# MLP up units in pairs by Strassen's scheme, with block sums of weights and tokens made on the chip

## The reference, cut to what matters

```python
def sqrelu_mlp(x, w_up, w_down):
    return jnp.square(jax.nn.relu(x @ w_up)) @ w_down
...
h = h + sqrelu_mlp(rmsnorm_2(h, mlp_norm[l]), w_up[l], w_down[l])
```

## Time and profile before

| | |
|---|---|
| median of 3 runs | 2758.52 us (2756.25 to 2761.14) |
| the profiled execution | 2754.03 us, its span 2752.3 us |
| granted TensorE clock | 0.998 of full speed |
| busy: PE, DVE, ACT, POOL | 99%, 44%, 39%, 48% |
| an up unit: 24 matmuls of 512 tokens | 5.44 us |
| a quarter of an MLP: 16 units | 87 us |
| HBM | 94 GB/s over the span |

### The profile page before, as it was taken

The page is one execution under the profiler, slowest core; times in us unless marked ns, Lnnn a source line. Parts: engine busy times, 40 slices in busy tenths (PEclk is TensorE's granted clock), DMA queues, the critical chain, the costliest instruction groups (busy, mean ns, idle before and its releaser), DMA issues.

```text
span 2752.3 us, 34320 instructions
## 1 busy us (share of the span) xinstructions
PE 2713.0 (99%) x12422; PEld 2208.7 (80%) x12422; DVE 1220.6 (44%) x1603; ACT 1062.5 (39%) x1566; POOL 1321.0 (48%) x1028
## 2 busy tenths in 40 slices
PE   9999999999999999999999999999999998999999
PEld 7777777888877788787888877788888876788887
DVE  6755555212258645555121268633324237443222
ACT  4444434322343444434222348423324338433222
POOL 5455445544464544455544465454444432354443
PEclk9999999999999999999999999999999999999999
DMA  4333322233332333322333322222233220223233
GB/s 144 93 102 97 99 92 84 93 100 97 95 101 94 98 100 100 100 92 85 96 96 100 99 93 92 90 94 99 92 99 122 85 77 16 69 92 100 93 97 99
DMA packets 72699, 259.16 MB, mean 94 GB/s; under 512 B 8192, under 2 KB 9088, under 8 KB 72448
## 3 DMA queue, kind: packets, MB, share of 16 engines
q1 hardware_dynamic: 71280, 254.17, 29.0%
q10 hardware_dynamic: 1296, 3.28, 0.3%
HBM read 255.31 MB, written 2.10 MB: 94 GB/s over the span
## 4 chain that ended last, share of the span: by engine, by line
PE 79%; DVE 7%; issue 6%; POOL 5%; ACT 2%; DMA 1%; POOLq 0%; DVEq 0%; SPq 0%
PE ps L902 25%; PE ps L904 24%; PE ps L903 24%; POOL w_lo L370 3%; POOL w_lo L368 2%; PE ps L1143 1%; DVE XS L1954 1%; DVE fb L1953 1%; ACT w_hi L433 1%; PE ps L1038 1%; DVE st L1518 1%; PE ps L1029 1%; PE ps L1387 1%; PE ps L1389 1%; PE ps L1388 1%
## 5 line engine op out<-in xcount | busy, mean ns | idle before, releaser
L368 POOL TENSOR_TENSOR w_lo<-w_raw,w_hi 128x512 fp32r<-128x512 f32 x476 | 631.5, 1327 | 1330.8 <-ACT w_hi L433 1330.2
L902 PE MATMUL ps<-H_hi,w_hi 128*128 128x512 f32 x2240 | 890.0, 397 | 12.2 <-POOL w_lo L370 5.7
L904 PE MATMUL ps<-H_hi,w_lo 128*128 128x512 f32 x2240 | 872.5, 390 | 0.0
L903 PE MATMUL ps<-H_lo,w_hi 128*128 128x512 f32 x2240 | 872.3, 389 | 0.0
L433 ACT ACTIVATE w_hi<-w_raw 128x1024 fp32r<-128x1024 f32 x476 | 499.6, 1055 | 556.1 <-DMA w_raw<-w_all 556.0
L370 POOL TENSOR_TENSOR w_lo<-w_raw,w_hi 128x512 fp32r<-128x512 f32 x476 | 655.1, 1376 | 0.0
L902 PEld LDWEIGHTS ps<-H_hi,w_hi 128*128 128x128 f32 x2240 | 420.6, 188 | 116.4 <-issue 13.4
L903 PEld LDWEIGHTS ps<-H_lo,w_hi 128*128 128x128 f32 x2240 | 420.7, 188 | 92.2 <-issue 7.4
L904 PEld LDWEIGHTS ps<-H_hi,w_lo 128*128 128x128 f32 x2240 | 420.5, 188 | 88.3
L902 PE MATMUL ps<-Y_hi,w_hi 128*128 128x512 f32 x1168 | 457.2, 391 | 7.5 <-DVE Y_lo L1666 2.8
L904 PE MATMUL ps<-Y_hi,w_lo 128*128 128x512 f32 x1168 | 454.7, 389 | 0.0
(11 more groups left out here) (278 smaller groups left out, 2477.7 us busy)
## 6 DMA issues: line engine op xcount, KB each, us to landing
w_raw<-w_all SPq DMA_DIRECT2D x476, 512.0 KB, 3.5
X<-xT SPq DMA_DIRECT2D x8, 256.0 KB, 5.5
rel_bias<-bias ACTq DMA_DIRECT2D x1, 2048.0 KB, 8.4
outT<-X SPq DMA_DIRECT2D x8, 256.0 KB, 3.2
sguw<-sgu_wT ACTq DMA_DIRECT2D x2, 256.0 KB, 3.1
CS<-cossin SPq DMA_DIRECT2D x1, 256.0 KB, 7.5
sgub<-sgu_b ACTq DMA_DIRECT2D x2, 128.0 KB, 3.0
sgug<-sgu_g ACTq DMA_DIRECT2D x2, 128.0 KB, 3.0
```

Source lines behind the costliest of these rows:

```text
L368: nc.gpsimd.tensor_tensor(w_lo[:, s, 0:UNIT // 2], w_raw[:, s, 0:UNIT // 2], f(w_hi[:, s, 0:UNIT // 2]), ALU.subtract).then_inc(w_lo_half, 1)
L902: MM(out, wh, xh, start=start, stop=False)
L903: MM(out, wh, xl, start=False, stop=False)
L904: return MM(out, wl, xh, start=False, stop=stop)
```

## The change

It pairs the up units. The tokens are cut into two halves of 256 (columns 1 and 2), the inputs into two halves of 512, and two up units are the two blocks of output features. For the pair, a 2 x 2 block product, eight half products (512 inputs, 128 features, 256 tokens) become seven, by the scheme with 15 block sums:

- Token sums (four blocks `T` of 512 inputs x 256 tokens, gain included) are made once for each MLP: `tokens_split` on ACT and `token_sums` on DVE after the output units, then `T_hi` on ACT (four instructions of 1024 columns), `T_lo` two on DVE and two on POOL.
- Weight sums (four of 512 columns for each pair: S1, S2, S4, S3, in two sets of buffers `E_raw`, `E_hi`, `E_lo`) are made on DVE by `weight_sum`, up to two pairs ahead, rounded on ACT by `hi_sum`, and their rest is made on POOL in `low_pair`, behind three halves of the pair's own weights. The fourth half is used only in sums.
- PE's `window` makes the seven products of 12 matmuls of 256 tokens: G, r, V (S1), r resumed (S2), then the cross product of the next pair (bank 4), V resumed (S4), r resumed (S3). Resuming adds on to a bank whose content has been copied out before: ACT copies four half banks (`copied`).
- DVE's `c11`, `c12` and `c2` add copies and banks to the four output blocks in `fa`; `linear` is ReLU and the factor `RS` in one instruction, ACT squares twice (to `XS`, and rounded to `Y_hi`), and DVE subtracts (`low`).

The cross product of a pair waits for `c11` of the pair before it, since they share bank 4. In the first quarter of each MLP the first four up units stay as they were, and pairs 2 and 3 follow. All else, down units included, stays, but the down units take the tiles of `Y` in the order in which they are now made.

```diff
+            def low_pair(n, U0, i, p):
+                u, q, c = unit_of(U0, i, 2 * p), pair_of(n, i, p), U0 + 2 * p
+                s2, s1 = c % WSLOTS, (c + 1) % WSLOTS
+                eng.wait_ge(w_hi_ready, u + 2)
+                eng.wait_ge(st_sum, q * 4 + 3)
+                nc.gpsimd.tensor_tensor(w_lo[:, s1, S:UNIT], w_raw[:, s1, S:UNIT], f(w_hi[:, s1, S:UNIT]), ALU.subtract).then_inc(w_lo_half, 1)
+                eng.wait_ge(st_sum, q * 4 + 4)
+                nc.gpsimd.tensor_tensor(w_lo[:, s2, S:UNIT], w_raw[:, s2, S:UNIT], f(w_hi[:, s2, S:UNIT]), ALU.subtract).then_inc(w_lo_half, 1)
+                nc.gpsimd.tensor_tensor(w_lo[:, s1, 0:S], w_raw[:, s1, 0:S], f(w_hi[:, s1, 0:S]), ALU.subtract).then_inc(w_lo_ready, 1)
+                for n_, o in enumerate((S1_, S2_, S4_, S3_)):
+                    if n_ < 3:
+                        eng.wait_ge(st_hi, q * 3 + (n_ + 1))
+                    nc.gpsimd.tensor_tensor(sums_of(E_lo, p, o), sums_of(E_raw, p, o), f(E_hi[:, p % 2, o:o + 1, :]),
+                                            ALU.subtract).then_inc(st_lo if n_ else w_lo_ready, 1)
...
+                for t in (1, 2):
+                    eng.wait_ge(t_hi, 4 * n + (3 if t == 1 else 4))
+                    nc.gpsimd.tensor_tensor(T_lo[:, t, :, :], T_raw[:, t, :, :], f(T_hi[:, t, :, :]), ALU.subtract).then_inc(t_lo_g, 1)
...
+                act.wait_ge(t_sum, n + 1)
+                for t in (3, 0, 1, 2):
+                    nc.scalar.activation(T_hi[:, t, :, :], T_raw[:, t, :, :], ACT.Copy).then_inc(t_hi, 1)
...
+                def ahead(i, p, part):
+                    if p < 4:
+                        if part == 0:
+                            hi_second(i, p)
+                        else:
+                            hi_first(i, p)
+                            hi_sum(i, p, S1_)
+                            hi_sum(i, p, S2_)
+                    elif p == 4:
+                        split_weights(unit_of(U0, i, 8 + part), U0 + 8 + part)
+                def window(i, p, first):
+                    if first:
+                        hi_second(i, p + 1)
+                        hi_first(i, p + 1)
+                        copied(i, p, COPY_G)
+                        copied(i, p, COPY_R1)
+                        hi_sum(i, p + 1, S1_)
+                        hi_sum(i, p + 1, S2_)
+                        copied(i, p, COPY_V)
+                        hi_sum(i, p + 1, S4_, 2)
+                    else:
+                        squared(i, p - 1, 0)
+                        copied(i, p, COPY_G)
+                        copied(i, p, COPY_R1)
+                        squared(i, p - 1, 1)
+                        copied(i, p, COPY_V)
+                        if p + 1 < 4:
+                            hi_sum(i, p + 1, S4_, 2)
+                    ahead(i, p + 2, 0)
+                    copied(i, p, COPY_R2)
+                    ahead(i, p + 2, 1)
...
+                def quarter(i, last):
+                    if first_pair(i):
+                        for j in range(4):
+                            u = U0 + j
+                            if j == 1:
+                                tick(u)
+                            elif j == 2:
+                                hi_second(i, 2)
+                                hi_first(i, 2)
+                            elif j == 3:
+                                hi_sum(i, 2, S1_)
+                                hi_sum(i, 2, S2_)
+                                hi_sum(i, 2, S4_, 2)
+                            act.wait_ge(w_used, u + 1)
...
+                def cross(i, p):
+                    u, q = unit_of(U0, i, 2 * p), pair_of(n, i, p)
+                    pe.wait_ge(w_lo_half, u + 1)
+                    if not isinstance(q, int) or q:
+                        pe.wait_ge(st_c, q * 2 - 1)
+                    half_product(BANK_Q, *slot_part(U0 + 2 * p + 1, 1), *half_of_h(4, 0))
...
+                def window(i, p, first):
+                    u, q = unit_of(U0, i, 2 * p), pair_of(n, i, p)
+                    r = bank_r(U0, p)
+                    if first:
+                        cross(i, p)
+                    pe.wait_ge(w_lo_half, u + 2)
+                    half_product(BANK_G, *slot_part(U0 + 2 * p, 1), *tokens(3)).then_inc(w_used, 1)
+                    pe.wait_ge(w_lo_ready, u + 1)
+                    pe.wait_ge(unit_out, u - 2)
+                    half_product(r, *slot_part(U0 + 2 * p + 1, 0), *half_of_h(0, 0)).then_inc(w_used, 1)
+                    pe.wait_ge(w_lo_ready, u + 2)
+                    if not isinstance(q, int) or q:
+                        pe.wait_ge(st_c, q * 2)
+                    half_product(BANK_V, *sum_part(p, S1_), *tokens(0)).then_inc(st_mm, 1)
+                    pe.wait_ge(st_lo, q * 3 + 1)
+                    pe.wait_ge(st_copy, q * 4 + 2)
+                    half_product(r, *sum_part(p, S2_), *tokens(1), fresh=False).then_inc(st_mm, 1)
+                    if p + 1 < 4:
+                        cross(i, p + 1)
+                    pe.wait_ge(st_lo, q * 3 + 2)
+                    pe.wait_ge(st_copy, q * 4 + 3)
+                    half_product(BANK_V, *sum_part(p, S4_), *half_of_h(4, 1), fresh=False).then_inc(st_mm, 1)
+                    pe.wait_ge(st_lo, q * 3 + 3)
+                    pe.wait_ge(st_copy, q * 4 + 4)
+                    half_product(r, *sum_part(p, S3_), *tokens(2), fresh=False).then_inc(st_mm, 1)
...
+            def token_sums(n, k):
+                g1, g2 = v(f"mlp{n}", k), v(f"mlp{n}", k + 4)
+                early, late = X[:, k + 4, 0:HS], X[:, k + 4, HS:S]
+                dve.wait_ge(t_raw, 4 * n + k + 1)
+                link(VE.scalar_tensor_tensor(T_raw[:, 0, k, :], X[:, k, HS:S], g1, T_raw[:, 0, k, :], ALU.mult, ALU.subtract))
+                VE.scalar_tensor_tensor(T_raw[:, 2, k, :], late, g2, T_raw[:, 2, k, :], ALU.mult, ALU.subtract)
+                link(VE.scalar_tensor_tensor(T_raw[:, 1, k, :], late, g2, T_raw[:, 0, k, :], ALU.mult, ALU.subtract))
+                i = VE.scalar_tensor_tensor(T_raw[:, 3, k, :], early, g2, T_raw[:, 1, k, :], ALU.mult, ALU.subtract)
+                if k == 3:
+                    i.then_inc(t_sum, 1)
...
+                    if not isinstance(q, int) or q >= 2:
+                        dve.wait_ge(st_mm, q * 4 + (o - 7))
+                    if o == S1_:
+                        dve.wait_ge(*loads(unit_of(U0, i, 2 * p), c))
+                        x = VE.tensor_tensor(s1, a21, a22, ALU.add)
+                    elif o == S2_:
+                        dve.wait_ge(*loads(unit_of(U0, i, 2 * p + 1), c + 1))
+                        dve.wait_ge(st_sum, q * 4 + 1)
+                        x = VE.tensor_tensor(s2, s1, a11, ALU.subtract)
+                    elif o == S4_:
+                        dve.wait_ge(st_sum, q * 4 + 2)
+                        x = VE.tensor_tensor(sums_of(E_raw, p, S4_), a12, s2, ALU.subtract)
+                    else:
+                        x = VE.tensor_tensor(sums_of(E_raw, p, S3_), a11, a21, ALU.subtract)
+                    x.then_inc(st_sum, 1)
...
+                def c11(i, p):
+                    q = pair_of(n, i, p)
+                    dve.wait_ge(st_copy, q * 4 + 2)
+                    VE.tensor_tensor(fa[:, 0, 0:HS], ps[:, BANK_Q, 0:HS], cp[:, COPY_R1, :], ALU.add).then_inc(st_c, 1)
...
+                    VE.scalar_tensor_tensor(fb[:, a, :], fa[:, a, :], 0.0, RS[:], ALU.max, ALU.mult).then_inc(st_lin, 1)
...
+                def window(i, p, first):
+                    if first:
+                        for o in (S1_, S2_, S4_, S3_):
+                            weight_sum(i, p + 1, o)
+                        c11(i, p)
+                    else:
+                        c2(i, p - 1)
+                        if p + 1 < 4:
+                            weight_sum(i, p + 1, S3_)
+                        linear(i, p - 1, 1)
+                        low(i, p - 1, 0)
+                        c11(i, p)
+                        low(i, p - 1, 1)
+                    if p + 2 < 4:
+                        for o in (S1_, S2_, S4_):
+                            weight_sum(i, p + 2, o)
+                    c12(i, p)
+                    linear(i, p, 0)
+                def ups(i):
+                    if first_pair(i):
+                        up(0)
+                        up(1)
+                        for o in (S1_, S2_, S4_, S3_):
+                            weight_sum(i, 2, o)
+                        up(2)
+                        up(3)
+                    for p in range(first_pair(i), 4):
+                        window(i, p, p == first_pair(i))
+                    c2(i, 3)
+                    linear(i, 3, 1)
+                    low(i, 3, 0)
+                    low(i, 3, 1)
...
+                        elif m == 6:
+                            hi_second(i + 1, 0)
+                            hi_first(i + 1, 0)
```

(19 more changed lines are left out.)

222 lines of the change are left out of this document (172 added, 50 removed).

## The result

The changed kernel takes 2805.23 us (2803.0 to 2805.42, four runs) against 2759.83 for the kernel before on the same chip, a ratio of 1.0164 (1.0151 to 1.0176). It is slower, as forecast, and inside the outer range (2738 to 2818), but by 45.4 us where the forecast said 26 and put its own ends at 10 and 40. The profiled executions differ by 51.4 us of span (2803.7 and 2752.3); the one of before was itself a short one, some 5 us under its median.

The account below looks back on a forecast made before the run. PE bounds the kernel before; with pairs, POOL and DVE taking turns stretch PE's windows. Steady quarters +6, first quarters +11 and +9 sum to +26 us (ends +10 and +40), about 2785 us; range 2738 to 2818.

Parts of the forecast that it names:

- the first quarters: First up part of each MLP: token work and late pairs delay PE, +11 us in MLP 0 and +9 in MLP 1.
- the term of the steady quarters: Three up parts per MLP after the first: 44.5 us for 43.5, +1.0 us six times, +6.
- PE's pace: Matmuls of 256 tokens in the pairs: 0.114 us each, a product 1.37 us, a pair 9.6.
- rival 5: Weight loads don't hide in the pairs: 0.225 us a matmul, a pair 18.9, +224 us, 2982; chance 0.02.
- The turn-taking: POOL and DVE steps with two SBUF operands alternate in the pairs: 1.70 us for one of each, at least 12.6 a pair.
- A steady quarter, step by step: Up part from PE's start: cross 1 at 7.5 us, c11 freeing cross 3 at 32.2, POOL's end 40.8, end 44.5.
- 2 (PE sets the pace): DVE reaches c11 before PE needs it; steady quarters 39.5 us, total -23, 2735; chance 0.20.
- 3 (48 us a steady quarter, 2813 in all): DVE's queue falls further behind: steady quarters +4.5 us each, first quarters +15 and +13, total +55; chance 0.20.
- the slack found was nil: End of a steady up part: last low parts of Y and first down unit's weights just covered, nothing to spare.
- POOL's steps: Sign in the pairs: steps of 1.74 us in most of a pair's seven; wrong if most stay at 1.29.
- the waits for `c11`: Sign in steady quarters: PE idle put down to DVE's c11 before cross products, and few other waits.
- the three waits of the first quarters: Sign in each MLP's first quarter: PE waits for POOL before the fourth unit and first pair, and for that pair's copies.

Follow-up runs that it names:

- `RS` in PSUM: Against the changed kernel, DVE copies RS once a quarter into a free PSUM bank, where the linear step reads it: 2779.84 us, 1.008 of before.
- POOL's narrow steps: Against the changed kernel, POOL's seven subtractions a pair cover 32 of 512 columns and PE's third matmul reuses the rounded weights: 2755.53 us, 0.9987 of before.
- the square in PSUM: Late pairs, late token splitting and RS in PSUM on the changed kernel, plus one of a pair's two squares in a free PSUM bank: 2751.96 us, 0.9981 of before.
- the two kernels that differ from it only in the first quarters: Changed kernel without pairs in the first quarters, 2794.14 us; the same with token splitting moved to the first quarter's down units, 2784.81 us.
- `c11` earlier: Against the changed kernel, DVE's c11 is moved ahead of the linear step and low part of the pair before: 2803.81 us, 1.0163 of before.

## Why the prediction was right, and where its sizes were off

The forecast said +26 us: 6 in the steady quarters, 20 in the first quarters, nothing elsewhere. In the traces it is +51.4 us of span: 21.0 in the steady quarters, 24.5 in the first quarters (9.6 and 11.2 in the up parts, 3.7 in the output units ahead of MLP 0) and 5.8 ahead of all that. So the direction, the mechanism and the first quarters came out; the term of the steady quarters is 3.5 times what was forecast, and by it the median's +45.4 lies above the forecast's own upper end of 40.

- **PE's pace: mis-sized.** I took 0.114 us a half matmul between ends of 0.109 and 0.120; it is the upper end. Rows of after, steady quarter:

```profile
1886.01 0.28 PE L1075 MATMUL ps<-H_hi,w_hi 128*128 128x256 f32 x1
1886.13 0.28 PE L1076 MATMUL ps<-H_lo,w_hi 128*128 128x256 f32 x1
1886.25 0.28 PE L1077 MATMUL ps<-H_hi,w_lo 128*128 128x256 f32 x1
```

A product is 1.44 us, not 1.37; the nine that follow the last cross product take 0.6 us more. The choice of half of 0.2267 was the error: the two paces lie 0.107 us apart, what 256 columns last at 2.4 GHz, and each is 0.013 us above its columns. Two paces don't show that this is a fixed part of each matmul (in the narrow case the loads, 0.111 apart in the earlier trace rows, come close too), but halving it was wrong. The loads do hide: a half matmul with a load of its own comes every 0.120 us, so rival 5 is out. That is against the sentence of the Trainium skill ("TensorE: Matmul & The Clock Gate", Part 3, The mechanism) by which loads overlap only when row groups differ; the same section also lets a load run ahead into a background weight buffer, and with that the rows agree.

- **The turn-taking: right in mechanism and price.** POOL's four `E_lo` in 6.84 us are 1.71 each, DVE's held steps 1.67 to 1.79, and 0.69 when one operand is in PSUM or POOL is out of the way. `RS` in PSUM, POOL's narrow steps and the square in PSUM each remove turns, from either side, and each time the quarter shortens. Who sets the end was right too. POOL's 21 steps of the later pairs begin at 1883.01, 5.7 us after PE's start at 1877.34 (forecast 5.6), and end at 40.6 (forecast 40.8), some 6 us ahead of PE; it is busy 44.96 us in the stretch because it goes straight on to the down units' weights. The 21 steps take 34.9 us, of which 21 x 1.24 = 26.0 are their own; the other 8.8 are 19 hold-ups of 0.46, where I counted 20. DVE's queue, with the copies of ACT hung into it, is the long one. The rows, with PE's first and the one that the last `c11` frees:

```profile
1877.34 0.28 PE L1075 MATMUL ps<-H_hi,w_hi 128*128 128x256 f32 x1
...
1883.01 1.69 POOL L444 TENSOR_TENSOR w_lo<-w_raw,w_hi 128x512 fp32r<-128x512 f32 x1 [1.35 <-DVE E_raw L2213]
...
1911.38 6.51 POOL L451 TENSOR_TENSOR E_lo<-E_raw,E_hi 128x512 fp32r<-128x512 f32 x4
...
1910.19 0.41 DVE L2221 TENSOR_TENSOR fa<-ps,cp 128x256 f32<-128x256 f32 x1
...
1910.65 0.38 PE L1075 MATMUL ps<-H_hi,w_hi 128*128 128x256 f32 x1 [1.98 <-DVE fa L2221]
```

- **A steady quarter, step by step** (from PE's start). First cross product forecast and measured at 7.5 (1884.84). Cross 2 measured at 19.7 (1897.08). The `c11` that frees cross 3 forecast at 32.2, measured at 33.3 (1910.19 + 0.41). End at 44.5 and 46.4. One reason of the slip is a load: pair 2's second half reached DVE at 1886.75, 1.51 us after DVE was ready for it, where I had it ready at once:

```profile
1886.75 1.44 DVE L2210 TENSOR_TENSOR E_raw<-E_raw,w_raw 128x512 f32<-128x512 f32 x1 [1.51 <-DMA w_raw<-w_all]
```

The steady quarters at full clock last 2.8 us over before instead of 1.0: 0.6 from the pace, the rest from the later chain. Over six that is +11.

- **The clock: missed.** PE has gaps now, and in three of the six steady quarters the granted clock fell, a term that the sum put at nothing without a reason. Five-microsecond stretches of the third quarter of MLP 0:

```profile
1985.00:1990.00 5.00, 3.16 (x19) 3.16 (x20) 4.97 (x5) 4.04 (x8) 5.00 (x4) 0.80 0.08 30
1990.00:1995.00 5.00, 5.00 (x38) 5.00 (x38) 4.93 (x5) 1.17 (x3) 5.00 (x4) 0.85 0.00 0
1995.00:2000.00 5.00, 3.67 (x31) 3.46 (x29) 5.00 (x6) 3.29 (x8) 5.00 (x4) 1.00 0.59 208
2000.00:2005.00 5.00, 4.58 (x26) 4.58 (x27) 1.77 (x4) 2.91 (x4) 5.00 (x4) 0.67 0.00 2
```

PE waits 1.92 us up to 1986.84, and the clock of the first stretch is 0.80, that is, part of it at the 1.2 GHz level; it waits 1.75 us up to 2000.42, and the fourth stretch is at 0.67. Only 26 matmuls lie in that one against 43 in a full one. These three quarters last 47.7 to 47.8 us and the others 46.3 to 46.4: 1.4 us each, 4 in all. The six have nearly the same waits for `c11` (two of 1.7 to 2.0 us each), so waits of this length do not always cost clock. Over all profiles: after and the two kernels that differ from it only in the first quarters have a wait of 1.9 us or more in each of their 18 steady quarters, and 9 of these ran at a mean of 0.93; in the five other kernels no wait in a steady quarter is over 1.3 us, and all 30 quarters ran at 1.00. With `c11` earlier the six are 3.9 us shorter than in after, of which the first quarters took back 2.3.

- **The first quarters: right, a little short.** With the 5.8 us by which the stage began late taken off (all from MLP 0): the last `H_lo` stalled PE by 1.9 us (forecast 2.0); the fourth unit's weights by 2.8 to 3.2 (2.6); the first cross product ran at 1806.54 - 5.8 = 1800.7 (1799.8); the copies of G and R1, 1817.01 to 1817.65, at 1811.2 to 1811.9 (R1 at 1811.1). The up part ended at 1828.0, with PE's first row of the down part at 1833.79, where I said 1826 (+13 for +11), at a mean granted clock of 0.91. That this MLP would pay more than the second did not hold in the up parts (9.6 and 11.2), only with the output units counted.

- **Rivals.** 2 (PE sets the pace) is what the narrow-POOL kernel shows; in the kernel as it is it is out. 3 (48 us a steady quarter, 2813 in all) lies nearer to the measured 46.3 to 47.8 and 2805 than the forecast's 44.5 and 2785 do: its reason, that the slack found was nil, held in part, and it had the first quarters too dear (28 us for 24.5). Both rest on the same mechanism, and by the number alone this rival comes nearer. The clock, which no rival had, carries 4 us. The late start is in the spans' 51.4 and not in the forecast's sum; without it they differ by 45.6, next to the 45.4 of the medians. Of the signs, POOL's steps, the waits for `c11` and the three waits of the first quarters came as named; POOL was busier than 90% (97%) and the up part longer than 44 to 45 us.

Not settled: whether the late start ahead of MLP 0 is wholly chance, and what decides in which quarters the clock falls. In the profiles of the other seven kernels the first add lies between 1737.19 and 1743.33, in the two of before at 1737.95 and 1746.71.

## What to carry to other kernels

A scheme that takes matmul work from PE must be costed by what it adds to the two engines beside it, not one by one but together: GpSimd and VectorE take turns when both read two SBUF operands, and a queue of such steps runs at 1.7 us each instead of 0.7. The last wait in PE's list names the place where the shortage surfaces, not its cause: a reordering moved the wait from DVE to ACT and POOL at the same total, while moving one operand into a free PSUM bank, at the price of one copy a quarter, took 25 us off, some 4 of them clock. And work that a new scheme needs once (here rounding the token sums) belongs in a stage where those engines have room: moved into the down units it cost nothing that the up parts show.
